# Window attention of a three-mixer model: merging the two key triangles of a query into one square

## The reference, cut to what matters

```python
WINDOW, A_KV_HEADS, A_GROUP, A_HEAD_DIM = 128, 4, 4, 64      # 16 query heads
scores = einsum('bnqkgd,bnskd->bnkgqs', q, kb) * A_HEAD_DIM ** -0.5   # kb: block before and own block, 256 keys
diff = qi + WINDOW - si
band = (diff >= 0) & (diff < WINDOW)
scores = where(band & (blk * WINDOW - WINDOW + si >= 0), scores, -inf)
m = maximum(max(scores, -1), sink)
e = exp(scores - m)
probs = e / (sum(e, -1) + exp(sink - m))
out = einsum('bnkgqs,bnskd->bnqkgd', probs, vb) @ w_o + b_o
```

## Time and profile before

| | us |
|---|---|
| median of 3 runs | 1476.51 (1475.95 to 1478.12) |
| profiled execution, its own time | 1476.34 |
| its span | 1474.2 |
| PE busy (matmuls) | 1464.1 (99%) |
| POOL busy | 902.5 (61%) |
| DVE busy | 710.0 (48%) |
| ACT busy | 440.6 (30%) |
| granted TensorE clock, mean | 1.000 |

### The profile page before, as it was taken

One profiled execution on the slowest core, in us unless ns is written; L12 is line 12 of the kernel. 1 busy time (PEld: TensorE's weight loads), 2 busy tenths in 40 slices (PEclk: granted clock), 3 DMA queues, 4 the chain that ended last, 5 costly groups with the idle time before them and its releaser, 6 DMA issues.

```text
span 1474.2 us, 19945 instructions
## 1 busy us (share of the span) xinstructions
PE 1464.1 (99%) x7232; PEld 1195.9 (81%) x7241; DVE 710.0 (48%) x864; ACT 440.6 (30%) x906; POOL 902.5 (61%) x719
## 2 busy tenths in 40 slices
PE   9999999999999999999999999999999999999999
PEld 7887777887888788888888888867888888888887
DVE  7764658430065785004532284776777300552253
ACT  3343584223232522001210054665152100221042
POOL 7766045866615597666776666811668666777653
PEclk9999999999999999999999999999999999999999
DMA  6332012333212233333233322301223323323322
GB/s 211 114 99 94 16 44 72 114 92 96 87 43 75 81 117 100 100 100 89 97 100 100 96 76 87 114 30 30 90 70 120 93 99 100 99 88 99 100 86 86
DMA packets 37315, 132.72 MB, mean 90 GB/s; under 512 B 4304, under 2 KB 4736, under 8 KB 37248
## 3 DMA queue, kind: packets, MB, share of 16 engines
q1 hardware_dynamic: 36576, 129.52, 27.9%
q10 hardware_dynamic: 672, 2.23, 0.4%
HBM read 129.59 MB, written 2.10 MB: 89 GB/s over the span
## 4 chain that ended last, share of the span: by engine, by line
PE 96%; ACT 2%; DVE 1%; DMA 1%; POOL 1%; issue 0%; SPq 0%; ACTq 0%
PE PS L647 22%; PE PS L649 22%; PE PS L648 22%; PE PS L598 2%; PE PS L599 2%; PE PS L580 2%; PE PS L941 2%; PE PS L1210 1%; PE PS L674 1%; PE PS L675 1%; PE PS L676 1%; PE PS L1033 1%; PE PS L1048 1%; PE PS L903 1%; PE PS L905 1%; PE PS L904 1%
## 5 line engine op out<-in xcount | busy, mean ns | idle before, releaser
L539 POOL TENSOR_TENSOR W_lo<-W_raw,W_hi 128x1024 fp32r<-128x1024 f32 x238 | 599.6, 2519 | 19.9
L536 POOL TENSOR_TENSOR HOLD<-HOLD 1x1 f32<-1x1 f32 x238 | 63.7, 268 | 536.0 <-PE PS L649 315.3
L647 PE MATMUL PS<-A_hi,W_hi 128*128 128x512 f32 x896 | 349.4, 390 | 0.1
L649 PE MATMUL PS<-A_lo,W_hi 128*128 128x512 f32 x896 | 348.7, 389 | 0.0
L648 PE MATMUL PS<-A_hi,W_lo 128*128 128x512 f32 x896 | 348.7, 389 | 0.0
L537 POOL TENSOR_SCALAR W_hi<-W_raw 128x1024 fp32r<-128x1024 f32 x238 | 248.0, 1042 | 0.0
L647 PE MATMUL PS<-H_hi,W_hi 128*128 128x512 f32 x512 | 199.2, 389 | 0.0
L648 PE MATMUL PS<-H_hi,W_lo 128*128 128x512 f32 x512 | 199.2, 389 | 0.0
L649 PE MATMUL PS<-H_lo,W_hi 128*128 128x512 f32 x512 | 199.2, 389 | 0.0
L647 PEld LDWEIGHTS PS<-A_hi,W_hi 128*128 128x128 f32 x896 | 168.2, 188 | 36.3 <-issue 0.8
L649 PEld LDWEIGHTS PS<-A_lo,W_hi 128*128 128x128 f32 x896 | 168.2, 188 | 35.1
(11 more groups left out here) (372 smaller groups left out, 2138.6 us busy)
## 6 DMA issues: line engine op xcount, KB each, us to landing
W_raw<-in_weights SPq DMA_DIRECT2D x238, 512.0 KB, 3.5
X<-in_x SPq DMA_DIRECT2D x4, 512.0 KB, 6.2
out<-X SPq DMA_DIRECT2D x7, 256.0 KB, 4.1
RELU<-in_ple_in ACTq DMA_DIRECT2D x2, 512.0 KB, 3.5
CONST<-in_constants ACTq DMA_DIRECT2D x1, 849.5 KB, 6.1
PARAM<-in_params SPq DMA_DIRECT2D x1, 320.5 KB, 8.6
SIN<-in_positions ACTq DMA_DIRECT2D x1, 256.0 KB, 3.4
out<-X SPq DMA_DIRECT2D x2, 128.0 KB, 1.7
```

What stands on the lines that cost most here:

```text
L536: pool.tensor_tensor(HOLD[:, 1 + s:2 + s], HOLD[:, 0:1], HOLD[:, 0:1], ALU.add)
L539: pool.tensor_tensor(W_lo[:, s, :], W_raw[:, r, :], W_hi[:, s, :].bitcast(F32), ALU.subtract).then_inc(w_lo, 1)
L647: pe.matmul(PS[:, bank, :], W_hi[:, slot, w], hi[:, kk, :], start=first, stop=False)
L649: done = pe.matmul(PS[:, bank, :], W_hi[:, slot, w], lo[:, kk, :], start=False, stop=last)
```

## The change

The mask products go. The scores of a group are written straight to PSUM; DVE then merges the two triangles: a `copy_predicated` with the constant `before_mul` (1 where r < c) as mask copies the block-before scores over the own-block scores, in PSUM, for both heads and blocks at once. For block 0 the block-before slot holds -1e30, set once. Maxima, exponents, transposes and copies then work on one 128 x 128 square for each head and block, 4 for each group. Since weights of both key blocks now lie in one square, the output is the merged weights times the values of the block before, plus the own-block triangle of the weights (`OWN3`, a product with `TRI`) times the difference of values (`V3_STEP`). POOL makes `V3_STEP`, `OWN3` for groups 0 to 14, and `A_hi` and `A_lo` for pairs 0 to 5; DVE makes `OWN3` of group 15; all copies to `PT3` are ACT's. POOL splits weights up to block 1 of `out3` (of 8) before this work and the others after it. The set-up of the masks moves from ahead of the rotation to between its tiles 7 and 8. In PE's queue the order of an iteration is transposes(g), spread, weigh(g-1), scores(g+2); in DVE's it is share(p-1), maxima(g+2), inverse(p), mix(p-1), the sinks of the next pair.

```diff
@@ set-up and queue of POOL
+            def window_attention():
+                stage_at = KD * A_STAGE["mixed3"]
+                pool.wait_ge(by_dve, PLAN["v3"].before + 2)
+                pool.tensor_tensor(V3_STEP[:], V3[:, 1:NT], V3[:, 0:NT - 1], ALU.subtract).then_inc(swa_stepped, 1)
+                for g in range(2 * SWA.pairs - 1):
+                    p, c = g // 2, g % 2
+                    cols, n = (slice(0, T), NT) if c else (slice(2 * P, T), 2)
+                    pool.wait_ge(SWA.read_by_act, g + 1)
+                    pool.tensor_tensor(OWN3[:, g % 2, cols].rearrange("p (n c) -> p n c", n=n),
+                                       PT3[:, g % 2, cols].rearrange("p (n c) -> p n c", n=n),
+                                       TRI[:].unsqueeze(1).broadcast_to([P, n, P]), ALU.mult).then_inc(swa_own, 1)
+                    if c and 0 < p < SWA.pairs - 1:
+                        k = p - 1
+                        pool.wait_ge(mix_ready, 3 * KD + k + 1)
+                        pool.tensor_scalar(A_hi[:, k, :], MIX[:, k % 2, :], 1.0, 1.0, ALU.mult, ALU.mult).then_inc(a_hi, 1)
+                        pool.wait_ge(a_hi, stage_at + k + 1)
+                        pool.tensor_tensor(A_lo[:, k, :], MIX[:, k % 2, :], A_hi[:, k, :].bitcast(F32),
+                                           ALU.subtract).then_inc(a_lo, 1)
+            splits(W_SLOTS, PLAN["out3"].first + 2)
+            window_attention()
+            splits(PLAN["out3"].first + 2, N_BLOCKS)
@@ queue of PE
-                    for h in range(2):
-                        pe.matmul(PS[:, score_bank(g, h), :], IDENT_B[:], WINDOW_B[:, 2 * c * P:2 * c * P + T], start=True,
-                                  stop=False, skip_group_check=True)
-                                           QK3[half, p // 4, first:first + width], start=False, stop=True,
+                                           QK3[half, p // 4, first:first + width], start=i == 2 * c, stop=True,
+                    if g == 0:
+                        pe.wait_ge(swa_stepped, 1)
+                    if g < 2 * SWA.pairs - 1:
+                        pe.wait_ge(swa_own, g + 1)
+                    else:
+                        pe.wait_ge(swa_own_last, 1)
+                    if c == 0 and p:
                         pe.wait_ge(mix_ready, 3 * KD + p)
+                    for s in range(2):
+                        i = 2 * c + s
+                        for j, (turned, values) in enumerate(((PT3, V3[:, max(i - 1, 0), p // 4, :]),
+                                                              (OWN3, V3_STEP[:, max(i - 1, 0), p // 4, :]))[0:2 if i else 1]):
                 for g in range(2 * SWA.pairs):
+                    transposes(g)
+                    if c == 0 and p:
+                        spread_inverse(SWA, p - 1)
                     if g:
+                        weigh(g - 1)
+                    if g + 2 < 2 * SWA.pairs:
                         scores(g + 2)
+                weigh(2 * SWA.pairs - 1)
@@ queue of ACT
+                for q in range(4):
+                    exponent(0, q)
+                for g in range(2 * SWA.pairs):
+                    n = g + 1
+                    if n < 2 * SWA.pairs:
+                        exponent(n, 0)
+                    copy(g)
+                    if n < 2 * SWA.pairs:
+                        for q in range(1, 4):
+                            exponent(n, q)
+                    if n % 2:
+                        act.wait_ge(SWA.sink_in, n // 2 + 1)
                         act.activation(SMALL[:, 8:16], SMALL[:, 8:16], ACT.Exp).then_inc(SWA.sinked, 1)
+                    else:
+                        widen(SWA, g // 2)
+                mixed(SWA.pairs - 2)
                 mixed(SWA.pairs - 1)
@@ queue of DVE
-                    dve.tensor_reduce(raw, PS[:, bank:bank + 2, :].rearrange("p b (s c) -> p b s c", s=2),
-                                      mybir.AxisListType.X, ALU.max).then_inc(SWA.scores_read, 1)
+                    dve.copy_predicated(score_slots(g, False), past, score_slots(g, True)).then_inc(swa_merged, 1)
+                    dve.wait_ge(swa_merged, g + 1)
+                    dve.tensor_reduce(raw, score_slots(g, False), mybir.AxisListType.X, ALU.max).then_inc(SWA.scores_read, 1)
+                    if c == 0 and p:
+                        share(p - 1)
+                    if g + 2 < 2 * SWA.pairs:
+                        maxima(g + 2)
+                    if c == 0:
+                        inverse(p)
+                    if c == 0 and p:
+                        mix(p - 1)
+                    if c and p + 1 < SWA.pairs:
+                        sinks(p + 1)
+                last = 2 * SWA.pairs - 1
+                dve.wait_ge(SWA.read_by_act, last + 1)
+                dve.tensor_tensor(OWN3[:, last % 2, :].rearrange("p (n c) -> p n c", n=NT),
+                                  PT3[:, last % 2, :].rearrange("p (n c) -> p n c", n=NT),
+                                  TRI[:].unsqueeze(1).broadcast_to([P, NT, P]), ALU.mult).then_inc(swa_own_last, 1)
+                    if i == 7:
+                        set_window()
```

More of the change, by code:

```diff
@@ L351, in build @@
         HALVES, HALF_BANKS = (slice(0, 2 * P), slice(2 * P, T)), (3, 5)
+        swa_merged, swa_own, swa_own_last, swa_stepped = (sem("swa_" + n) for n in ("merged", "own", "own_last", "stepped"))
         rope_swapped, roped, window_set = sem("rope_swapped"), sem("roped"), sem("window_set")
@@ L546, in _, with splits @@
                 split(n, n, n // RAW_SLOTS)
[L547 to L551, removed]
+            def splits(first, last):
+                whole, part = -(-first // W_SLOTS), last // W_SLOTS
+                for n in range(first, whole * W_SLOTS):
+                    split(n, n % W_SLOTS, n // RAW_SLOTS)
+                with pool.Fori(whole, part) as g:
+                    for s in range(W_SLOTS):
+                        split(g * W_SLOTS + s, s, g * uses + s // RAW_SLOTS)
+                for n in range(part * W_SLOTS, last):
+                    split(n, n % W_SLOTS, n // RAW_SLOTS)
+            def window_attention():
[19 more added lines that the diff above has]
+            splits(PLAN["out3"].first + 2, N_BLOCKS)
         @block.tensor
@@ L1041, in transposes @@
[L1041 to L1044, removed]
-                    else:
-                        pe.wait_ge(by_dve, PLAN["v3"].before + v + 1)
-                    for at in range(0, 2 * SWA.width(v), P):
-                        mm = pe.transpose(PS[:, 6 + v % 2, at:at + P], PR3[:, v % 4, at:at + P], const("ident"))
+                def transposes(g):
+                    pe.wait_ge(SWA.exped, 4 * (g + 1))
+                    if g >= 2:
+                        pe.wait_ge(SWA.read_by_act, g - 1)
+                    else:
+                        pe.wait_ge(by_dve, PLAN["v3"].before + g + 1)
+                    for at in range(0, T, P):
+                        mm = pe.transpose(PS[:, 6 + g % 2, at:at + P], PR3[:, g % 2, at:at + P], const("ident"))
@@ L1062, in window_attention @@
                 for g in range(2 * SWA.pairs):
[L1063 to L1066, removed]
+                    p, c = g // 2, g % 2
+                    transposes(g)
+                    if c == 0 and p:
+                        spread_inverse(SWA, p - 1)
                     if g:
[L1068 to L1072, removed]
+                        weigh(g - 1)
+                    if g + 2 < 2 * SWA.pairs:
                         scores(g + 2)
-                weigh(SWA.steps - 2)
-                weigh(SWA.steps - 1)
+                weigh(2 * SWA.pairs - 1)
                 spread_inverse(SWA, SWA.pairs - 1)
@@ L1529, in mixed @@
                 def mixed(p):
+                    act.wait_ge(a_hi, KD * A_STAGE["mixed3"] + p)
                     act.wait_ge(mix_ready, 3 * KD + p + 1)
[L1531 to L1539, removed]
+                    act.activation(A_hi[:, p, :], MIX[:, p % 2, :], ACT.Copy).then_inc(a_hi, 1)
@@ L1541, in exponent, with copy @@
                                    accum_out=sum_columns(p)[:, at:at + 1]).then_inc(SWA.exped, 1)
[L1543 to L1548, removed]
-                for g in range(2 * SWA.pairs):
[L1551 to L1563, removed]
+                def copy(g):
+                    act.wait_ge(SWA.turned, g + 1)
+                    if g >= 2:
+                        act.wait_ge(SWA.weighed, g - 1)
+                    act.activation(PT3[:, g % 2, :], PS[:, 6 + g % 2, :], ACT.Copy).then_inc(SWA.read_by_act, 1)
@@ L1567, in window_attention @@
-                copy(SWA.steps - 2)
-                widen(SWA, SWA.pairs - 1)
+                    else:
+                        widen(SWA, g // 2)
+                mixed(SWA.pairs - 2)
                 mixed(SWA.pairs - 1)
@@ L2149, in window_attention @@
                     p, c = g // 2, g % 2
[L2150 to L2155, removed]
-                    if c == 0 and p:
-                        inverse(p - 1)
```

(13 more changed lines are left out.)

63 lines of the change are left out of this document (32 added, 31 removed).

## The result

The changed kernel takes 1484.93 us (median of five runs, 1483.73 to 1486.20) against 1476.51 (1475.95 to 1478.29): ratio 1.0054, 95% interval 1.0044 to 1.0065. It is 8.4 us slower. The forecast was 1479.6, and the range ended at 1483.6. The sign was the likelier one; the size was missed by 5.3 us.

A forecast was written before the change was run, and what follows sets the result against it. The prediction took PE to bound the kernel before, and a loop of hand-overs after. Head -1.1, loop +1.3 and tail +2.85 gave +3.05 us on 1476.51, so 1479.6; range 1475.6 to 1483.6.

The forecast's parts named there:

- The loop: Hand-overs from transposes(2p) through DVE's merge, maxima, inverse and mix to weigh(2p): 7.57 us a pair against 7.35, +1.3 in all.
- PE's need: PE's own work in a pair of heads falls from 7.35 to 5.4 us without mask products and six transposes.
- The merge: DVE's predicated copy from PSUM to PSUM: 0.70 us, lower bound 0.35, upper bound 1.22.
- POOL's 3.9 a pair: POOL's new work in a pair, OWN3 for both groups plus A_hi and A_lo: 3.9 of 7.57 us.
- The lock: POOL and DVE instructions with two SBUF inputs exclude each other: cost 0 in the loop; delays inverse and OWN3(15) at the end.
- Rival (b): The merge costs 1.22 us, 0.52 more in each of six periods: +6.7, 1483.2 us; chance 0.14.
- (a): POOL's weight splitting misses the tail, which is only 0.5 us longer: sum +0.7, 1477.2 us; chance 0.20.
- The head: Start of the stage, up to transposes(2): shorter scores but weigh(0) waiting for POOL, -1.1 us.
- The tail: From transposes(14) to the output product: inverse and OWN3(15) on DVE wait for POOL's weight splitting, +2.85 us.
- Rival (d): PE's idle bits drop its clock to 1.2 GHz, doubling its work over seven pairs: +33, 1510 us; chance 0.03.
- signs of being wrong: A period under 7.3 or over 7.8 (merge or loop), OWN3(15) at 0.65 (lock), clock under 1.00 in the stage.
- Rival (c): weigh(2p) does not wait for mix(p-1); the exponents' loop rules at 6.3 us a pair: -4.5, 1472.0 us; chance 0.08.

The follow-up runs named there:

- e9: e1 with the merge of every even group (c = 0) done twice; 1483.22 us, ratio 1.0047.
- e12: The changed kernel, no idle products, with the merge of every even group (c = 0) done twice; 1492.21 us, ratio 1.0107.
- e2: The changed kernel with POOL waiting for DVE's OWN3 of the last group before it splits the remaining weight blocks; 1479.78 us, ratio 1.0021.
- e1: The changed kernel with idle products in PE's waits, around odd groups' transposes and before the last weighing; 1478.18 us, ratio 1.0011.
- e3: The changed kernel with mix(p-1) directly behind share(p-1) in DVE's queue, ahead of the maxima; 1478.58 us, ratio 1.0013.
- e7: e4 with POOL's A_lo also waiting until the maxima of group 2p+3 are done; 1470.95 us, ratio 0.9964.
- e11: The changed kernel, no idle products, with the merge of every odd group (c = 1) done twice; 1484.85 us, ratio 1.0059.
- e4: The changed kernel with both e2's and e3's edits; 1475.37 us, ratio 0.9994.
- e6: The changed kernel with both e1's and e2's edits; 1478.77 us, ratio 1.0014.
- e8: e7 with idle products at the end alone, three ahead of transposes(15), six ahead of the last weighing; 1471.91 us, ratio 0.9968.
- e10: e1 with the merge of every odd group (c = 1) done twice; 1482.62 us, ratio 1.0044.

## Why the prediction was wrong

**Right, by its own steps.** The loop: 7.57 predicted, 7.54 measured, by the links named, and doubling the even merge lengthens it by just 0.73 (e9; in e12, where the clock blurs the period, PE's idle time grows by 0.73). PE's need of 5.4 a pair: 5.50. The merge, 0.70, and the reduction, 0.69. POOL's 3.9 a pair: 3.86. The lock, twice: OWN3(15) on DVE from 5.4 to 7.6 on the tail's clock (5.7 to 7.95 predicted), gone in e2. Rival (b) is out by the row, (a) by the trace; e2 makes what (a) describes, and comes out 2.6 above (a)'s 1477.2, of which the clock's 3.4 in the loop is more than all.

**Off in size.** The head gave 1.55, not 1.1. The tail at full clock comes to 10.37 - 0.96 - 0.61 = 8.8, which is +2.0 instead of +2.85. Of that 0.85, 0.3 is OWN3(15), done 7.64 after T(14) and not 7.95; another 0.24 is that the prediction took the output product's start before the change from the timeline (1019.06), but added up the new one link by link, as the chain counts, and the chain has 1019.30. So -1.55 + 1.1 + 2.0 = +1.5, where the sum said +3.05, and an error of 1.5 the other way hid as much of what follows. e1, which runs at full clock, stands 1.9 above its own before.

**The step that failed** is the clock: the forecast's sum holds no term for it, that is, it let PE wait 2 us of every 7.5 at full speed. Rival (d) named the right mechanism with a chance of 0.03, and with a price, +33, that assumed a clock low in the whole loop. It is neither all nor nothing: PE runs at full clock throughout the first two of the six pairs, at half for some 3 us twice in the other four, each time across the border of two, and for some 7 us behind the last wait. That is 6.5 us, and with the +1.5 makes +8.0 of the measured 8.4. The reason against it, "clock 1.00 in every stretch that I asked for", spoke of a PE that hardly waits; the prediction said so itself, and still priced only the clock that is low throughout. The trace of before has one stretch with waits, the first 10 us, PE busy 7.12 of 10 at clock 1.00; it would have looked harmless, as the changed kernel's pair from 976.26 does. A clock under 1.00 in the stage was among the prediction's signs of being wrong, and it came; it also made the pairs of over 7.8, another of these signs, which the prediction had meant for the merge or the loop. A case in between, 3 to 8 us as the traces now have it (3 to 5 in the loop, up to 3 at the end), would have moved the range's upper end to where the result lies. The Trainium skill ("TensorE: Matmul & The Clock Gate", section "A second HAM failure mode: psum-queue depth-cycling") tells of a kernel whose clock oscillates between the two levels because PE idles for short bits between groups of products. The changed kernel's trace agrees: three falls to a granted clock of 0.50 in this stage, with waits of 2.0 us at most.

**Rival (c)** does not happen in the changed kernel, but its loop is real. With the mix moved forward it gave 7.33 (e3), and without A_lo's lock 6.80 (e7), where 6.3 was worked out. The first 0.53 is shown by e7. The other 0.5 is in the sum: (c) followed the odd groups. The chain of e7 follows the even ones, with the spread (0.52) and the longer weighing (1.02, not 0.81), less 0.18 for shorter scores.

**Open.** Which of PE's waits makes the clock fall, and why in other pairs from run to run, isn't settled. The pairs from 976.26 and from 983.80 have the same work and the same waits to 0.03 us up to the mix, and only in the second does the clock fall. And e11 leaves PE idle a little longer in a pair than the changed kernel does (2.19 against 2.04), and lost no more (2.9). So the idle time in a pair doesn't decide it alone; only that filling it ends the loss (e1), and that longer waits at the even merge raise it (e12), is shown. Each loss in the table is that of one trace.

## What to carry to other kernels

Taking work off the busiest engine pays only as far as the next loop of hand-overs allows; lay out one period in queue order, and read how much of the next engine's work stands between a result and the one that waits for it. Then price the holes too: TensorE, made to wait twice in each period where it never waited, can lose its clock there at times, and the loss belongs in the range as a middle case, not as all or nothing. Give GpSimd's new work a place in time as carefully as its length: a single wait ahead of one of its instructions gave 5.2 us (e2 against the changed kernel) and 4.4 us (e7 against e4), and only with both of them and the mix moved forward did the change gain anything.

## What the runs showed that was not expected

- Idle products made the kernel 6.8 us faster (e1), at a full clock; where they stand in front of work that is ready they delay it. From T(14) to the output product it took 9.13 with them and 7.32 without (e6, e2), 7.15 and 6.43 (e8, e7); a pair with the odd merge doubled took 8.30 and 7.69 (e10, e11).
- The lock catches the smallest instructions: an operation on four columns took 1.23 us behind A_lo (e3) and 0.62 behind A_hi, which reads one operand only (e7), instead of 0.16. The Trainium skill ("SBUF — State Buffer", section "Who interferes with whom") says that a VectorE instruction with two SBUF inputs contends with a GpSimd instruction that reads SBUF; the A_hi row agrees.
- A predicated copy of 128x512 from PSUM to PSUM with its mask in SBUF took 0.70 us, no more than one operation with two operands.
